# First chunk of the first feed-forward part: block by block with both row groups

## The reference

```python
def swiglu(x, w_gate, w_up, w_down):
    return (jax.nn.silu(x @ w_gate) * (x @ w_up)) @ w_down
...
    for i in range(DEPTH):
        h = swiglu(x, ffn_w_gate[i, 0], ffn_w_up[i, 0], ffn_w_down[i, 0])
        x = layer_norm(ALPHA * x + 0.5 * h, ln_g[i, 0], ln_b[i, 0])
        ...
        x = layer_norm(ALPHA * x + y, ln_g[i, 1], ln_b[i, 1])
        h = swiglu(x, ffn_w_gate[i, 1], ffn_w_up[i, 1], ffn_w_down[i, 1])
        x = layer_norm(ALPHA * x + 0.5 * h, ln_g[i, 2], ln_b[i, 2])
```

## Time and profile before

| | us |
|---|---|
| median of 3 runs | 1000.98 (1000.14 to 1001.07) |
| span of the profiled execution, first to last instruction | 998.0 |
| PE busy in the span | 983.0 |
| DVE busy | 571.9 |
| ACT busy | 444.5 |
| POOL busy | 44.7 |

### The profile page before, as it was taken

How to read it: one execution, slowest core, us unless ns; L and a number is a source line. 1 busy time by engine, 2 the same in 40 slices (tenths; PEclk the granted TensorE clock), 3 DMA queues, 4 the chain that set the end, 5 groups by cost and what they waited for, 6 DMA issues and landing times.

```text
span 998.0 us, 13263 instructions
## 1 busy us (share of the span) xinstructions
PE 983.0 (98%) x5158; PEld 826.3 (83%) x5158; DVE 571.9 (57%) x624; ACT 444.5 (45%) x507; POOL 44.7 (4%) x72
## 2 busy tenths in 40 slices
PE   9999999999999999999999999999999999999996
PEld 7888888899987888888888888889888678888885
DVE  5555463766557555554665554547576585445634
ACT  5443452357653444352254434534565443344430
POOL 1100000000001000000000000001121110000000
PEclk9999999999999999999999999999999999999999
DMA  9956546456633756546565565654554436564521
GB/s 319 290 185 194 199 174 220 166 182 225 211 114 90 247 169 196 188 172 243 169 211 168 180 198 197 225 174 154 180 196 142 127 124 210 181 201 168 210 85 43
DMA packets 136951, 182.80 MB, mean 183 GB/s; under 512 B 5936, under 2 KB 120784, under 8 KB 136912
## 3 DMA queue, kind: packets, MB, share of 16 engines
q1 hardware_dynamic: 134032, 173.56, 52.6%
q0 software_dynamic: 2592, 8.17, 2.6%
q10 hardware_dynamic: 288, 0.52, 0.2%
HBM read 181.16 MB, written 1.07 MB: 183 GB/s over the span
## 4 chain that ended last, share of the span: by engine, by line
PE 91%; DVE 5%; POOL 1%; issue 1%; ACT 1%; DMA 0%; POOLq 0%; SPq 0%; DVEq 0%
PE psum L356 28%; PE psum L358 28%; PE psum L357 28%; PE psum L393 2%; DVE stick L909 2%; PE psum L516 1%; PE psum L526 1%; POOL stick L1026 1%; PE psum L537 1%; PE psum L344 1%; DVE probs L916 1%; DVE stats L819 1%; DVE x L839 1%; DVE x L816 1%; ACT stick L693 1%
## 5 line engine op out<-in xcount | busy, mean ns | idle before, releaser
L773 DVE TENSOR_TENSOR w_lo<-raw,w_hi 128x2048 fp32r<-128x2048 f32 x162 | 368.8, 2287 | 158.0 <-ACT w_hi L605 157.5
L605 ACT ACTIVATE w_hi<-raw 128x2048 fp32r<-128x2048 f32 x162 | 303.0, 1907 | 89.5 <-PE psum L358 87.8
L356 PE MATMUL psum<-w_hi,xT_hi 128*128 128x512 f32 (+1 forms) x832 | 317.2, 381 | 0.7 <-DVE w_lo L782 0.7
L358 PE MATMUL psum<-w_hi,xT_lo 128*128 128x512 f32 (+1 forms) x832 | 310.9, 374 | 0.0
L357 PE MATMUL psum<-w_lo,xT_hi 128*128 128x512 f32 (+1 forms) x832 | 310.4, 373 | 0.0
L356 PEld LDWEIGHTS psum<-w_hi,xT_hi 128*128 128x128 f32 x832 | 156.7, 188 | 29.8 <-DVE w_lo L782 1.8
L358 PEld LDWEIGHTS psum<-w_hi,xT_lo 128*128 128x128 f32 x832 | 156.5, 188 | 28.3
L357 PEld LDWEIGHTS psum<-w_lo,xT_hi 128*128 128x128 f32 x832 | 156.9, 189 | 25.9
L356 PE MATMUL psum<-w_hi,hT_hi 128*128 128x512 f32 x416 | 164.3, 395 | 0.0
L358 PE MATMUL psum<-w_hi,hT_lo 128*128 128x512 f32 x416 | 162.1, 390 | 0.0
L357 PE MATMUL psum<-w_lo,hT_hi 128*128 128x512 f32 x416 | 162.0, 390 | 0.0
(11 more groups left out here) (71 smaller groups left out, 512.2 us busy)
## 6 DMA issues: line engine op xcount, KB each, us to landing
raw<-in_ffn_w_down SPq DMA_DIRECT2D x88, 512.0 KB, 4.1
raw<-in_ffn_w_gate SPq DMA_DIRECT2D x86, 512.0 KB, 4.0
raw<-in_ffn_w_up SPq DMA_DIRECT2D x86, 512.0 KB, 5.0
raw<-in_w_qkv_a SPq DMA_DIRECT2D x24, 512.0 KB, 4.7
raw<-in_w_qkv_b SPq DMA_DIRECT2D x24, 512.0 KB, 4.5
raw<-in_w_o_a SPq DMA_DIRECT2D x8, 512.0 KB, 4.1
raw<-in_w_o_b SPq DMA_DIRECT2D x8, 512.0 KB, 3.7
gain<-in_ln_g POOLq DMA_DIRECT2D x6, 512.0 KB, 3.9
```

The costliest lines, as they stand in the source:

```text
L356: pe.matmul(acc, st[0], mv[0], start=first, stop=False)
L358: return pe.matmul(acc, st[1], mv[0], start=False, stop=last)
L605: act.activation(w_hi[slot][:], raw[raw_slot][:], ACT.Copy).then_inc(hi_done, 1)
L773: dve.tensor_tensor(w_lo[slot][:], raw[raw_slot][:], w_hi[slot][:], ALU.subtract).then_inc(lo_done, 1)
```

## The change

It has five parts.

1. Chunk 0 is computed block by block: for each block both row groups, by the new function `gate_up_first`, in place of half passes by row group. The table's product stands before block 6. The release of the loading slots comes at the ends of blocks 3 and 7.
2. The transposes of a piece are issued for both row groups together: piece 0 before block 0, piece 1 before block 1, piece 2 before block 3. They get six PSUM banks of their own.
3. x is loaded in three pieces, each with both row groups, by ACT's queue. SP loads only weights there: blocks 0 and 1 one at a time, then pairs.
4. ACT and DVE take for each of the first three weight parts first the weights, then the piece of x of both row groups.
5. The warm-up is 12 matmuls on a zeroed tile that DVE sets, ahead of the first transposes, in place of 6, 1 and 1 on the identity matrix.

```diff
-EARLY = [(0, 0, 1), (0, 1, 2), (0, 2, 3), (0, 3, 4), (1, 0, 2), (1, 2, 4)]
-WARM_UP = [6, 1, 1]
+EARLY = [(0, 0, 1), (0, 1, 2), (0, 2, 4), (1, 0, 2), (1, 2, 4)]
+WARM_UP = 12
+FIRST_TURNS = [(1, 1), (3, 2)]
+TABLE_AT = 6
...
+                for i, (n, a, b) in enumerate(EARLY):
+                    for w, at in ((w_gate, 0), (w_up, CHUNK_F)):
+                        src = w[0, 0, (4 * n + a) * P:(4 * n + b) * P, 0:CHUNK_F]
+                        sp.dma_start(as_gu(raw[n])[:, a:b, at:at + CHUNK_F],
+                                     src.rearrange("(k p) n -> p k n", p=P)).then_inc(early_raw(i), 16)
...
+            def transpose_first(piece):
+
+                pe.wait_ge(x_loaded[piece], 16)
+                a, b = PIECES[piece]
+                for r in range(ROWS):
+                    for k in range(a, b):
+                        last = pe.transpose(XT_first(r, piece)[:, (k - a) * P:(k - a + 1) * P],
+                                            x[:, r, k * P:(k + 1) * P], ident[:])
+                    last.then_inc(xT_psum, 1)
...
+            def gate_up_first():
+
+
+                for kk in range(KD):
+                    n, k = divmod(kk, 4)
+                    for at, piece in FIRST_TURNS:
+                        if at == kk:
+                            transpose_first(piece)
+                    if kk == TABLE_AT:
+                        relative_table()
+                    early_wait(pe, kk, early_lo, lo_done)
+                    for r in range(ROWS):
+                        xT_ready(0, r, kk)
+                        rows = slice(r * P, (r + 1) * P)
+                        last = three(GU[0][r], (xT_hi[:, kk, rows], xT_lo[:, kk, rows]),
+                                     (as_gu(w_hi[n])[:, k, :], as_gu(w_lo[n])[:, k, :]), kk == 0, kk == KD - 1)
+                        if r == 0 and kk == KD - 1:
+                            last.then_inc(gu_done, 1)
+                    if k == 3:
+                        last.then_inc(unit_used, 1)
...
-                    gate_up(0, 0, 0, n0, False, t, [(3, 0), (3, 1)], khs=(0,))
-                    gate_up(1, 0, 0, n0, True, t, khs=(0,))
-                    transpose_x(t, 1, (2,))
-                    gate_up(0, 0, 0, n0, False, t, khs=(1,)).then_inc(gu_done, 1)
-                    relative_table()
-                    gate_up(1, 0, 0, n0, True, t, khs=(1,)).then_inc(unit_used, 1)
+                    gate_up_first()
...
-            for pieces, count in zip(((), (0, 1), (2,)), WARM_UP):
-                transpose_x(0, 0, pieces)
-                for _ in range(count):
-                    pe.matmul(Y[1][1][:, 0:P], ident[:], ident[:], start=True, stop=True)
+            pe.wait_ge(warm_set, 1)
+            for _ in range(WARM_UP):
+                pe.matmul(Y[1][1][:, 0:P], hidden[:, 0, 0:P], hidden[:, 0, 0:P], start=True, stop=True)
+            pe.wait_ge(const_ready, 2)
+            transpose_first(0)
...
-            for half in range(2):
-                cols = slice(half * HALF, (half + 1) * HALF)
-                act.dma_start(x[:, 0, cols], x_in[0, 0:P, cols]).then_inc(x_loaded[half], 16)
+            for piece, (a, b) in enumerate(PIECES):
+                act.dma_start(x[:, :, a * P:b * P],
+                              x_in[0, :, a * P:b * P].rearrange("(r p) d -> p r d", p=P)).then_inc(x_loaded[piece], 16)
             act.wait_ge(const_ready, 1)
             load_table(ACT.Silu)
...
+            for piece in range(PARTS):
+                hi_early((piece,))
+                for r in range(ROWS):
+                    xT_hi_part(0, r, (piece,))
+            hi_early(range(PARTS, len(EARLY)))
...
+            dve.memset(hidden[:, 0, 0:P], 0.0).then_inc(warm_set, 1)
+            for piece in range(PARTS):
+                lo_early((piece,))
+                for r in range(ROWS):
+                    xT_lo_part(0, r, (piece,))
+            lo_early(range(PARTS, len(EARLY)))
```

More of the change, by code:

```diff
@@ L166, in XT, with XT_first, xT_count @@
             return psum[:, 4 + piece, 0:(b - a) * P]
+        def XT_first(r, piece):
+            a, b = PIECES[piece]
+            return psum[:, (4, 5, 6)[piece] if r == 0 else (7, 2, 3)[piece], 0:(b - a) * P]
+        def xT_count(t, r, piece):
+            return ROWS * piece + r + 1 if t == 0 else (ROWS * t + r) * PARTS + piece + 1
         SCORES = psum[:, 0:2, 0:KEYS]
@@ L177, in build @@
         hi_done, lo_done, unit_used = sem("hi_done"), sem("lo_done"), sem("unit_used")
-        early_loaded = [sem(f"early_loaded{n}") for n in range(2)]
+        early_loaded = [sem(f"early_loaded{i}") for i in range(3)]
         early_hi, early_lo = sem("early_hi"), sem("early_lo")
@@ L202, in build @@
         const_set, const_ready = sem("const_set"), sem("const_ready")
+        warm_set = sem("warm_set")
         stored = sem("stored")
@@ L215, in as_rows, with early_raw @@
             return t[:].rearrange("p (k n) -> p k n", k=2)
+        def early_raw(i):
+            n, a, b = EARLY[i]
+            return raw_loaded[n] if b == 4 else early_loaded[sum(x[2] < 4 for x in EARLY[:i])]
         def early_wait(eng, k, early, done):
@@ L334, in transpose_x @@
                 for piece in pieces:
[L335 to L338, removed]
+                    pe.wait_ge(x_ready, ((t - 1) * ROWS + r) * PARTS + piece + 1)
                     if r > 0:
@@ L351, in xT_ready @@
                     if a == k:
-                        pe.wait_ge(xT_lo_done, (ROWS * t + r) * PARTS + piece + 1)
+                        pe.wait_ge(xT_lo_done, xT_count(t, r, piece))
             def three(acc, st, mv, first, last):
@@ L358, in three, with gate_up @@
                 return pe.matmul(acc, st[1], mv[0], start=False, stop=last)
[L360 to L367, removed]
+            def gate_up_first():
[16 more added lines that the diff above has]
+                        last.then_inc(unit_used, 1)
+            def gate_up(r, par, slot, n, release, t=None, between=()):
+                for kh in range(2):
                     s = (slot + kh) % 4
-                    if not release and not static_zero(n):
+                    if not release:
                         unit_ready(n + kh)
@@ L372, in gate_up @@
                         kk = 4 * kh + k
-                        if static_zero(n) and not release:
-                            early_wait(pe, kk, early_lo, lo_done)
                         for at, piece in between:
@@ L611, in hi_early @@
             def hi_early(parts):
-                for n, a, b in parts:
-                    if a % 2 == 0:
-                        act.wait_ge((early_loaded[n], raw_loaded[n])[a // 2], 32)
+                for i in parts:
+                    n, a, b = EARLY[i]
+                    act.wait_ge(early_raw(i), 32)
                     act.activation(as_gu(w_hi[n])[:, a:b, :], as_gu(raw[n])[:, a:b, :],
@@ L638, in xT_hi_part @@
                     a, b = PIECES[piece]
-                    act.wait_ge(xT_psum, (ROWS * t + r) * PARTS + piece + 1)
+                    act.wait_ge(xT_psum, xT_count(t, r, piece))
+                    xt = XT(piece) if t > 0 else XT_first(r, piece)
                     act.activation(xT_hi[:, a:b, r * P:(r + 1) * P],
-                                   XT(piece).rearrange("p (k n) -> p k n", n=P), ACT.Copy).then_inc(xT_hi_done, 1)
+                                   xt.rearrange("p (k n) -> p k n", n=P), ACT.Copy).then_inc(xT_hi_done, 1)
             def ffn_scalar(f, t):
@@ L800, in xT_lo_part @@
                     a, b = PIECES[piece]
-                    dve.wait_ge(xT_hi_done, (ROWS * t + r) * PARTS + piece + 1)
+                    dve.wait_ge(xT_hi_done, xT_count(t, r, piece))
                     dst = (slice(None), slice(a, b), slice(r * P, (r + 1) * P))
-                    dve.tensor_tensor(xT_lo[dst], XT(piece).rearrange("p (k n) -> p k n", n=P), xT_hi[dst],
+                    xt = XT(piece) if t > 0 else XT_first(r, piece)
+                    dve.tensor_tensor(xT_lo[dst], xt.rearrange("p (k n) -> p k n", n=P), xT_hi[dst],
                                       ALU.subtract).then_inc(xT_lo_done, 1)
```

## The result

| | before | changed |
|---|---|---|
| median of 5 runs, us | 1000.54 (1000.14 to 1001.07) | 1004.92 (1004.71 to 1005.23) |
| span of the profiled execution, us | 998.0 | 1002.7 |
| first matmul of chunk 0 (F), us | 7.64 | 7.34 |
| first matmul of chunk 1 (T, T'), us | 21.75 | 24.67 |

The changed kernel is slower: ratio 1.0043, 95% interval 1.0031 to 1.0055. That is 4.4 us by the medians and 4.7 by the spans; 0.2% would be 2.0 us. The forecast was 1005.8, with a span of 1002.8. The first matmul of chunk 1 comes 2.92 us later than before.

A forecast was written before the change was run, and what follows sets the result against it. PE, busy for 983.0 of 998.0 us, was taken as the bound. Delays of 2.95 and 1.84 us made +4.8, a span of 1002.8, and with 2.98 around it 1005.8 us; range 1003.0 to 1007.0.

The forecast's parts named there:

- The end of chunk 0: First matmul of chunk 1 comes at 24.7 us instead of 21.75, +2.95 us.
- The round trips: PE waits before blocks 2 and 4, 1.5 and 1.75 us, as weight copies queue behind xT_hi of pieces 1 and 2.
- Unit 3: In chunk 1, PE waits 1.73 us for unit 3's w_lo, copied behind silu and table; +1.84 with restart.
- Rival (d): Later work absorbs half or more of the delay: below +2.0 us, or an accidental gain; chance 0.06.
- (c): PE's idle spells let the clock fall, twelve matmuls at half speed, +2.7 us: 1008.5; chance 0.06.
- Rival (b): Not slower: copies go at the pace weights land, so no waits before blocks 2 and 4: 1000.8 us; chance 0.08.
- The first matmul: Start of chunk 0: first matmul at 7.8 us, set by 24 warm-up passes of 5.3 us; range 6.7 to 8.0.
- rival (a): Same waits, but the clock rises within the warm-ups, first matmul at 6.7 us: +3.7, 1004.7; chance 0.30.
- The loads: Costed at nothing: at 2.9 us per MB, x and blocks 0 to 3 in by about 9.2 us, before ACT wants them.
- S: Moment in chunk 0 when the transposes of x piece 2 start, put at E + 4.8 us.
- E: Moment in chunk 0 when the transposes of x piece 1 may start, put 1.48 us after the first matmul.
- The surround: Time outside the profiled span, 2.98 us (median 1000.98 against span 998.0), assumed to stay.

The follow-up runs named there:

- turns_early: Changed kernel with the transposes of x piece 1 moved before block 0 and of piece 2 before block 1: 1001.85 us, ratio to before 1.0011.
- moves_pair: Changed kernel, transposes of pieces 1, 2 before blocks 0, 1, unit 3's copy before silu, blocks 0 and 1 loaded as a pair: 999.91 us, ratio 0.9992.
- moves_x2: Changed kernel, unit 3 copied before silu, x piece 2 loaded behind blocks 2 and 3, transposes before blocks 0 and 2: 999.29 us, ratio 0.9986.

## Why the prediction was right

- **The end of chunk 0.** T' was put at 24.7 and came at 24.67, +2.92 against T. The forecast was +2.95.
- **The round trips.** The waits before blocks 2 and 4 were put at 1.5 and 1.75. From one matmul's start to the next the gaps of PE are 1.63 (10.90 to 12.53) and 1.96 (16.05 to 18.01), less a step of 0.23: 1.40 and 1.73. (The brackets, 1.23 and 1.57, count from the modelled end of the matmul before.) The second round trip took 18.01 - 14.03 = 3.98 against 4.0 worked out from four transposes. Moving the transposes alone removed 3.1 us (turns_early), which shows the cause.
- **Unit 3.** w_hi was put at T' + 0.18, w_lo at T' + 2.12, PE at T' + 4.47. They came at + 0.17, + 2.10 and + 4.44. The wait was put at 1.73 and came at 1.72 (29.11 - 27.16 - 0.23). With the restart it was put at 1.84, and the edit that takes it away is worth 1.84 by the medians; agreement to the last digit is chance, since these differences carry some tenths.
- **Nothing later takes it back.** 2.92 + 1.84 = 4.76, and the spans differ by 4.7. Rival (d) did not happen, nor (c): steps between matmuls stay 0.23 behind each wait. Rival (b) was shown false by the copy at 15.63, which waited only for the xT_hi ahead of it, and by turns_early, where the copies came early once the transposes did. (Its sum has a slip: it puts F at 6.2, where midway between 5.7 and 7.6 is 6.65, which gives 1001.2 instead of 1000.8. Nothing hangs on it.)
- **The first matmul, mis-sized.** "I take F = 7.8"; it came at 7.34. The 24 passes took 5.93 - 1.12 = 4.81 us, not 5.3, since the last of them already ran at full clock, as rival (a) had it in part. PE started at 1.12, put at 1.05. In the six profiles with 12 warm-ups and block 0 loaded alone, F went from 6.82 to 7.75, so the prediction was right to give F a range.
- **The loads, mis-sized.** "By that pace x and blocks 0 to 3 (2.1 MB) are in by about 9.2", and hence the copy of blocks 2 and 3 was taken as bound by order alone. Block 1's copy waited for its load until 8.23, and that of blocks 2 and 3 until 10.16, where the order allowed 8.81 + 0.96 = 9.77. So S came 5.2 behind E, not 4.8. That 0.4 and the 0.46 of F cancel, which made T' better than its terms. The wait before block 2 is lucky in the same way: the round trip took 12.53 - 8.81 = 3.72 us instead of 3.3, but 0.39 of that PE had already stood before block 1 (9.64, where 8.81 + 0.44 = 9.25 was possible), whose w_lo was late with its load. The windows view of 2 to 6 us (busy us and count of each engine, granted clock, DMA share, GB/s) has this row in the kernel before:

```profile
2.00:6.00 4.00, 4.00 (x20) 3.87 (x20) 0.42 (x1) 1.62 (x3) 1.83 (x7) 1.00 0.94 316
```

and this in the changed kernel, 18% less traffic:

```profile
2.00:6.00 4.00, 4.00 (x23) 4.00 (x23) 0.00 (x0) 2.11 (x3) 1.83 (x7) 1.00 0.83 260
```

Which of the loads' changes lowers it is not settled: the pair of moves_pair did not bring it back (261), and with x piece 2 behind it was 287 to 289.
- **The surround, mis-sized.** The sum used 2.98 us around the span, the median of the runs less one execution's span. In the changed kernel the profiled execution took 1004.71 with a span of 1002.7, so 2.0, and every execution whose span is on record has 1.8 to 2.1. The other 1.0 us of the term is how far the median of three runs lay above the profiled execution of the kernel before; for the changed kernel it is 0.2 (1004.92 against 1004.71). With 2.0 the forecast would be 1004.8. This term, not a stage, is most of the 0.9 us between 1005.8 and 1004.92.

## What to carry to other kernels

Working block by block over two row groups covers a wait for weights only if the next blocks' copies are not queued behind results of the current block; issue the transposes ahead of the work that has to cover their round trip through two other engines (two numbers in a list were worth 3.1 us here). Before a result is moved later, look at what stands behind its reader in the same list and how much time that has to spare: here an unrelated copy had 0.87 us, and came 1.7 us late. And a sum made on a span needs the time around that same execution, or an error of its own for it.

## What was not expected of the hardware

- The moment at which the warm-up passes speed up differs between executions of like starts: 24 passes took 4.45 us (moves_x2), 4.87, 4.97, 5.15, 5.31, 5.38 and 5.49 (moves_pair). All began at 1.12 or 1.13 us. The Trainium skill (TensorE: Matmul & The Clock Gate, on the warm-up) says that the rise depends on a counter which does not start with the kernel; by that rule such a spread is to be seen. The traces agree with it as far as they go: they show the spread, not its cause, and have one execution of each of seven kernels, which are alike on PE up to there.
- With 12 warm-ups every profile had the short step from the first matmul on (6.8 to 8.1 us). With 6, and with idle spells of 0.78 and 0.99 us behind them, it stayed at 0.43 us a matmul up to 12.6 us. The column of the granted clock read full speed in all of them, so matmul steps are the thing to read.
